# Storing the up projection's split activations in reverse token order and streaming them backwards

## The reference, cut to what matters

```python
def conv_glu_ffn(h, w_up, w_conv, w_down):
    up = causal_dwconv(h @ w_up, w_conv)      # (256 x 2048) @ (2048 x 11264), width-3 causal convolution over tokens
    g, u = jnp.split(up, 2, axis=-1)
    return (jax.nn.silu(g) * u) @ w_down      # (256 x 5632) @ (5632 x 2048)
...
x = x + conv_glu_ffn(rmsnorm(x, norm_ffn[l]), ffn_up[l], ffn_conv[l], ffn_down[l])
```

## Time and profile before

| what | value |
|---|---|
| median of 3 runs | 2098.74 us (2098.2 to 2099.31) |
| the profiled execution, its own time | 2098.79 us |
| its span, first to last instruction | 2096.6 us |
| TensorE busy | 2052.9 us, 98% of the span |
| VectorE busy | 1229.7 us, 59% |
| ScalarE busy | 895.7 us, 43% |
| mean granted TensorE clock | 0.992 of full speed |

### The profile page before, as it was taken

One profiled execution on the slowest core, in us unless ns is written; L12 is line 12 of the kernel. 1 busy time (PEld: TensorE's weight loads), 2 busy tenths in 40 slices (PEclk: granted clock), 3 DMA queues, 4 the chain that ended last, 5 costly groups with the idle time before them and its releaser, 6 DMA issues.

```text
span 2096.6 us, 36640 instructions
## 1 busy us (share of the span) xinstructions
PE 2052.9 (98%) x15803; PEld 1983.2 (95%) x15803; DVE 1229.7 (59%) x1312; ACT 895.7 (43%) x864; POOL 34.0 (2%) x44
## 2 busy tenths in 40 slices
PE   5999999999999999999999999999999999999998
PEld 5999999999999999999999999888888888899998
DVE  5477644543544457577474445677877777744443
ACT  4444433344446443355444434544444444433332
POOL 2000000000000000000000000000000000000000
PEclk8999999999999999999999999999999999999999
DMA  7555444366455865656565355656555655556563
GB/s 220 162 177 190 137 133 134 111 205 200 151 172 176 299 198 189 213 161 190 177 194 163 121 160 166 218 178 200 188 179 193 200 181 180 181 199 194 188 195 125
DMA packets 358511, 377.43 MB, mean 180 GB/s; under 512 B 11913, under 2 KB 354723, under 8 KB 357123
## 3 DMA queue, kind: packets, MB, share of 16 engines
q1 hardware_dynamic: 354771, 353.36, 52.9%
q0 software_dynamic: 3632, 22.42, 2.9%
HBM read 364.75 MB, written 11.01 MB: 179 GB/s over the span
## 4 chain that ended last, share of the span: by engine, by line
PE 95%; DVE 2%; ACT 1%; issue 1%; DMA 0%; POOL 0%; SPq 0%; DVEq 0%; ACTq 0%
PE bank L1701 22%; PE bank L1703 22%; PE bank L1702 22%; PE bank L1735 15%; PE bank L1737 8%; PE bank L1912 1%; PE bank L1859 1%; DVE w_lo L974 1%; PE bank L2115 1%; PE bank L2096 1%; ACT w_hi L457 0%; DVE tmp L1018 0%; DVE x_home L1024 0%; PE bank L1846 0%; PE bank L1778 0%
## 5 line engine op out<-in xcount | busy, mean ns | idle before, releaser
L974 DVE TENSOR_TENSOR w_lo<-raw,w_hi 128x2048 fp32r<-128x2048 f32 (+1 forms) x352 | 763.8, 2170 | 630.3 <-ACT w_hi L457 629.8
L457 ACT ACTIVATE w_hi<-raw 128x2048 fp32r<-128x2048 f32 (+1 forms) x354 | 644.1, 1820 | 1105.8 <-PE bank L1703 827.3
L1701 PE MATMUL bank<-x_home,w_hi 128*128 128x256 f32 x2304 | 653.1, 283 | 18.3 <-DVE x_home L1024 15.2
L1703 PE MATMUL bank<-x_home,w_lo 128*128 128x256 f32 x2304 | 648.0, 281 | 0.0
L1702 PE MATMUL bank<-x_home,w_hi 128*128 128x256 f32 x2304 | 646.9, 281 | 0.0
L1735 PE MATMUL bank<-x_home,w_hi 128*128 128x512 f32 x1408 | 488.7, 391 | 3.6 <-DVE x_home L1583 2.2
L1701 PEld LDWEIGHTS bank<-x_home,w_hi 128*128 128x128 f32 x2304 | 436.2, 189 | 21.0 <-issue 13.3
L1702 PEld LDWEIGHTS bank<-x_home,w_hi 128*128 128x128 f32 x2304 | 437.0, 190 | 0.2
L1703 PEld LDWEIGHTS bank<-x_home,w_lo 128*128 128x128 f32 x2304 | 436.1, 189 | 0.0
L1737 PE MATMUL bank<-x_home,w_lo 128*128 128x256 f32 x1408 | 397.6, 282 | 0.0
L1735 PEld LDWEIGHTS bank<-x_home,w_hi 128*128 128x128 f32 x1408 | 264.4, 188 | 59.4 <-DVE xT L988 1.7
(11 more groups left out here) (279 smaller groups left out, 2182.9 us busy)
## 6 DMA issues: line engine op xcount, KB each, us to landing
raw<-in_w_in SPq DMA_DIRECT2D x53, 2048.0 KB, 8.6
raw<-in_ffn_up SPq DMA_DIRECT2D x44, 2048.0 KB, 8.0
raw<-in_ffn_down SPq DMA_DIRECT2D x32, 1408.0 KB, 6.5
raw<-in_xa_wkv SPq DMA_DIRECT2D x16, 2048.0 KB, 8.9
raw<-in_w_br SPq DMA_DIRECT2D x8, 2048.0 KB, 8.3
raw<-in_w_out SPq DMA_DIRECT2D x8, 2048.0 KB, 8.7
raw<-in_xa_wq SPq DMA_DIRECT2D x8, 2048.0 KB, 8.1
raw<-in_xa_wo SPq DMA_DIRECT2D x8, 2048.0 KB, 8.1
```

What stands on the lines that cost most here:

```text
L457: return nc.scalar.activation(out_, in_, func, **kw)
L974: tt(split_out(w_lo, kind, half), halves(raw, kind, half, par), split_out(w_hi, kind, half).bitcast(f32), ALU.subtract).then_inc(lo_ready, 1)
L1701: mm(o, w[0], x[0], start=start, stop=False)
L1703: return mm(o, w[1], x[0], start=False, stop=stop)
```

## The change

Three places: the high parts and the low parts of `x_up` are written with the tokens in reverse order within each group (the source `xg` is read in rising order, the destination has a step of -1), and both matmuls of the up projection read them with a step of -1 from the last element of the group, so that the columns arrive in the order of the tokens as before. PSUM is written in rising order, as before. Everything behind it is unchanged.

```diff
             def upper_residual(c):
                 act.wait_ge(x_g, c + 1)
-                copy(x_up[:, 0, 2 * c:2 * c + 2, :], xg[:, 2 * c:2 * c + 2, :]).then_inc(n_hi, 1)
+                copy(x_up[:, 0, 2 * c:2 * c + 2, ::-1], xg[:, 2 * c:2 * c + 2, :]).then_inc(n_hi, 1)
...
             for c in range(8):
                 dve.wait_ge(n_hi, 13 + c)
-                tt(x_up[:, 1, 2 * c:2 * c + 2, :], xg[:, 2 * c:2 * c + 2, :], x_up[:, 0, 2 * c:2 * c + 2, :].bitcast(f32),
+                tt(x_up[:, 1, 2 * c:2 * c + 2, ::-1], xg[:, 2 * c:2 * c + 2, :], x_up[:, 0, 2 * c:2 * c + 2, ::-1].bitcast(f32),
                    ALU.subtract).then_inc(n_lo, 1)
...
                         o = up_bank(par, half)
-                        mm(o[:, :].rearrange("p (j s) -> p j s", j=2), w_hi[:, half, k * P:(k + 1) * P], acts[:, :, k, :],
+                        mm(o[:, :].rearrange("p (j s) -> p j s", j=2), w_hi[:, half, k * P:(k + 1) * P], acts[:, :, k, ::-1],
                            start=k == 0, stop=False)
-                        last = mm(o[:, SEQ:2 * SEQ], w_lo[:, half, k * P:(k + 1) * P], acts[:, 0, k, :], start=False, stop=k == KC - 1)
+                        last = mm(o[:, SEQ:2 * SEQ], w_lo[:, half, k * P:(k + 1) * P], acts[:, 0, k, ::-1], start=False, stop=k == KC - 1)
```

## The result

The changed kernel takes 2103.41 us (median of 9 runs, 2101.92 to 2104.75); the kernel before, measured beside it, 2098.2 us (9 runs, 2096.05 to 2099.78). The ratio is 1.0026 with a 95% interval of 1.0017 to 1.0035: slower by 5.2 us, a little over the 0.2% that was called measurable.

A forecast was written before the change was run, and what follows sets the result against it. The prediction took TensorE's streaming of columns in the up projection as the bound. Matmuls, writes and the rest each counted zero against the profiled 2098.79 us, giving 2098.8 us, no change, with a range of 2090.5 to 2113.

The forecast's parts named there:

- What bounds the stage: Up projection: TensorE streaming its columns sets the pace, busy 50 of 50 us; 1408 pairs take 488 us.
- The writes: Eight ScalarE copies and eight VectorE subtractions storing backwards, 4.4 and 5.0 us: taken as zero, upper end +5.0 us.
- The rival of slow writes: Reversed writes are slow: +5.0 us at the start of the stage, 2103.8 us; chance 0.06.
- The rest: Weight loads keep their direction and PSUM its order, L1603 and the taps find the same tile: zero.
- The term of the 2816 matmuls: Backward reading at L1735 and L1737 in the up projection: taken as zero, between -8.0 and +13.9 us.
- the likeliest case: No change in the whole kernel's time, 2098.8 us, own range 2094.6 to 2103; chance 0.42.
- The bounds: Limits for 4224 backward runs at L1735 and L1737: -1.9 to +3.3 ns a run, from other stages' paces.
- The rival of dearer starts: First elements of 4224 runs at L1735 and L1737 cost 1.7 to 3.3 ns more: +7 to +14 us; chance 0.26.
- The rival of cheaper starts: Up projection takes the down projection's pace: -5 to -8 us, 2091 to 2093.5 us; chance 0.15.
- Half rate: Backward matmul streams lose pairing of rising elements and fall to plain float32 pace: +424 us, 2523 us; chance 0.08.
- The gain of 31 us: Up projection's excess over two cycles' pace goes away, a pair at 0.325 us: -31 us, 2068 us; chance 0.03.

The follow-up runs named there:

- the adjacent layout: Kernel before with each group's low run directly behind its high run, so L1735 reads 512 elements in one piece: 2096.78 us beside 2096.90.
- byte 0: The x_up view at byte 0 of its tile instead of 32: kernel before (forward) 2107.91 us, changed kernel (backward) 2105.66, beside 2094.51.
- the mixed halves: Two of four halves in one kernel, view at byte 32: only L1737 backward in one, only L1735 in the other; 2098.88 us beside 2098.23.
- the forward sweep: Forward reading with the view at bytes 16, 48, 80 and 96, one in each half of a loop step: 2100.91 us, kernel before 2097.89.

## Why the prediction was right or wrong

**What bounds the stage: right.** TensorE's stream, nobody else: the idle times, the clock of 1.00 and the other engines' busy times stand as they did, and what TensorE lost, ScalarE waited.

**The writes: right at zero**, 4.4 and 5.0 us before and after. The rival of slow writes is out.

**The rest at zero: right for what the change does**; the same 36640 instructions, and in the stage's groups only L1735 grew.

**The term of the 2816 matmuls: taken as zero, measured +6.2 us.** This is the step that failed, and with it the point forecast: the time, 2103.41 us, is in the stated range of 2090.5 to 2113 but just outside the likeliest case's own, 2094.6 to 2103. The argument for zero was that a run of 256 elements "holds the same bytes from either side, and it starts and ends at the same two boundaries". The runs show that the two directions aren't alike: at the same byte they differ by 0 to 6.7 ns a pair. The bounds, taken from the spread of pace between the kernel's other stages (-8.0 and +13.9 us), were of the right size: the forward kernels span 346.7 to 353.3 ns, 9 us over 1408 pairs.

That the time lies in the range is in part luck, for the bounds rested on a reading that doesn't hold. The prediction put the differences between the stages, up to 3.3 ns a matmul, down to "where a stream starts and what it meets", and took the down projection's pace from a stretch at 1899.85 us. In the same trace that stage ran slower up to 1884 us. The kernel before, and under it the kernel after, where no instruction of that stage was changed (timeline of PE, 40 groups each):

```profile
1850.14 0.28 PE L1701 MATMUL bank<-act_hl,w_hi 128*128 128x256 f32 x1
...
1864.54 0.28 PE L1701 MATMUL bank<-act_hl,w_hi 128*128 128x256 f32 x1
```

```profile
1850.09 0.28 PE L1701 MATMUL bank<-act_hl,w_hi 128*128 128x256 f32 x1
...
1864.09 0.28 PE L1701 MATMUL bank<-act_hl,w_hi 128*128 128x256 f32 x1
```

14.40 / 40 = 360 ns in the one and 14.00 / 40 = 350 in the other: 120.0 and 116.7 ns a matmul, the prediction's slowest and fastest stage, both in one untouched stage. In the kernel before TensorE pauses at 1884 us and goes on at 350 ns a group. This is also why the end of the kernel after is 0.5 us shorter: some 120 groups ran 10 ns faster, 1.2 us, and the first groups of the stage took part of it back.

**The rival of dearer starts, chance 0.26,** came nearest: +7 to +14 us was its price, +6.2 the stage's. Its mechanism, a surcharge on the first elements of each of 4224 runs, isn't borne out. Removing one run start in three (the adjacent layout) changed nothing forwards, and there is no surcharge in most halves at byte 0 and none in the mixed halves.

**The rival of cheaper starts, chance 0.15: out.** No kernel's pair went below 346.7 ns in a settled half. (Its -5 us would have been 2093.8 us, not 2093.5.)

**Half rate, chance 0.08: out.** From L1735 to L1737 it is 233.1 ns with the operand read backwards, not twice 228.4. The rule of the Trainium skill, "SBUF — State Buffer", section "Door 1: The DMA port swizzle", that accesses within a 16-byte line run at full bandwidth, agrees with these rows as far as the rate goes, to about 2%; it says nothing on the 4.6 ns.

**The gain of 31 us** from losing the excess over the columns, chance 0.03: no kernel or half settled below 346.7 ns a pair, 26.7 above its 768 columns at 2.4 GHz. That excess didn't yield to direction, to place or to adjacency.

**What stays open.** The runs don't settle why the pair takes 346.7, 351.1 or 353.3 ns. The pair with only L1735 backward ran at 346.7 in one kernel and 353.3 in another, and the forward pair at byte 0 at both paces in one execution: a stream keeps a pace into which it fell, so what went before it seems to have a part in which one that is. That direction and place have a part too is likely: at byte 32 every settled half that had both operands forward and the weights in place ran at 346.7 (the mixed ones did so too), and every half of the changed kernel from the second on at 351.1, in two layouts. But the comparisons between bytes, between directions at other bytes, and with the weights moved, are single executions that also differ in what goes before, so none of them gives a price for its one cause. No run changed only what goes before. Whether the changed kernel can also run at another pace is open for the same reason. Weights streamed in the other order were not tried.

## What to carry to other kernels

A reversed operand was not expensive here: writes cost nothing more, and the matmul stream lost 1.3%. But a stage that is nothing but back-to-back float32r matmuls can run at paces 2 or 3% apart, with no wait and no idle time; the sign in the profile is the distance of the starts. Read that distance over some 30 matmuls before and after any change of layout, and at several places of the stage, because the same instructions may change pace on the way. A difference of this size between two stages, or between two kernels in one execution each, isn't yet the effect of an offset or a direction: see first whether it holds through the whole stage and in a second execution.

## What the runs showed of the hardware that wasn't expected

The settled paces lie on steps. Starts repeat in a pattern of one, two, three or four pairs (or groups), and each whole pattern is, within the nanosecond of the trace, a multiple of 6.67 ns, 16 cycles at 2.4 GHz: one pair of 346.67 (52 steps) or 353.33 (53); the changed kernel's three pairs, 350, 351 and 352, together 1053.3 (158); the forward kernel at byte 0, whose pairs mostly go 350, 350, 360, 1060 (159); a half of the forward sweep (byte 48) with 346 and 354 in turn, 700 (105). One step a pair is 9.4 us of this kernel, and two thirds of one is what the change cost.

A stream can hold more than one of these paces with nothing about its instructions changed, and keep it for 30 us and more: 346.7 and 353.3 ns a pair in the forward kernel at byte 0, 360 and 350 ns a group in the down projection of the kernels before and after. That is more than turning the stream round cost.
